# Expert scatter split by columns, residual loaded while routing, combination reordered

## The reference

```python
h = rms_norm(x1, g_pre_ffn) * (1.0 + sc2) + sh2
# group = top 1 of 4, experts = top 2 of the 8 in it, weights from two softmaxes
# the 4096 (token, expert) pairs are sorted by expert, each expert padded to rows of 128
hb = silu(xb @ w_gate[e]) * (xb @ w_up[e])       # one block of 128 rows, 1024 -> 256
yb = (hb @ w_down[e]) * weight                   # 256 -> 1024
y[token] += yb                                    # each token receives two rows
out = x1 + gt2 * rms_norm(y, g_post_ffn)
```

## Time and profile before

| | us |
|---|---|
| three runs | 1723.42, 1720.57, 1712.91 |
| median | 1720.57 |
| the profiled execution | 1719.75 |
| its span in the trace | 1717.9 |
| mixer | 0 to 1110 |
| routing | 1110 to 1149 |
| experts, to the last scatter's landing | 1149 to 1672.6 |
| combination | 1672.7 to 1717.9 |

### The profile page before, as it was taken

One profiled execution on the slowest core, in us unless ns is written; L12 is line 12 of the kernel. 1 busy time (PEld: TensorE's weight loads), 2 busy tenths in 40 slices (PEclk: granted clock), 3 DMA queues, 4 the chain that ended last, 5 costly groups with the idle time before them and its releaser, 6 DMA issues. The chain is left out here.

```text
span 1717.9 us, 23909 instructions
## 1 busy us (share of the span) xinstructions
PE 1551.8 (90%) x7453; PEld 1162.1 (68%) x7454; DVE 1234.7 (72%) x1928; ACT 867.7 (51%) x1512; POOL 373.9 (22%) x395
## 2 busy tenths in 40 slices
PE   2699987999999999999999999838799999999974
PEld 2588976688956788855889665425577667767741
DVE  4589676469884589885598954385778877887737
ACT  2323262333374423474324343325778877887746
POOL 1000000100001100001000011113566666665640
PEclk8699876999999999999999989859899999999996
DMA  9343334223332332332332343289999997789959
GB/s 331 116 147 99 98 122 172 70 78 98 99 107 90 98 96 92 121 99 74 87 98 74 122 123 111 84 275 348 304 297 311 302 312 224 201 245 285 282 108 383
DMA packets 200420, 291.25 MB, mean 170 GB/s; under 512 B 10558, under 2 KB 158171, under 8 KB 200346
## 3 DMA queue, kind: packets, MB, share of 16 engines
q1 hardware_dynamic: 170720, 197.15, 34.5%
q0 software_dynamic: 29360, 92.99, 19.8%
q10 hardware_dynamic: 266, 0.14, 0.0%
HBM read 240.42 MB, written 59.26 MB: 174 GB/s over the span
## 5 line engine op out<-in xcount | busy, mean ns | idle before, releaser
L934 DVE SCALAR_TENSOR_TENSOR cv<-u,taps,cv 128x512 f32<-128x512 f32 x480 | 321.8, 746 | 0.1
L1764 DVE TENSOR_TENSOR w_rest<-wgu,w_high 128x1024 fp32r<-128x1024 f32 x192 | 234.3, 1222 | 94.7 <-ACT w_high L1687 90.1
L1687 ACT ACTIVATE w_high<-wgu 128x1024 fp32r x192 | 202.1, 1054 | 106.2 <-PE pgu L1641 87.9
L488 PE MATMUL bank<-wo,yT 128*128 128x512 f32 x512 | 228.1, 602 | 2.5 <-ACT hT L664 2.5
L461 PE MATMUL bank<-hT_high,tiles_operand 128*128 128x512 f32 x512 | 201.0, 393 | 9.8 <-DVE hT_operand L907 8.5
L462 PE MATMUL bank<-hT_operand,tiles_operand 128*128 128x512 f32 x512 | 200.2, 391 | 0.0
L463 PE MATMUL bank<-hT_high,win_operand 128*128 128x512 f32 x512 | 200.1, 391 | 0.0
L488 PEld LDWEIGHTS bank<-wo,yT 128*128 128x128 f32 x512 | 97.2, 193 | 119.0 <-issue 119.0
L1651 PE MATMUL py<-wd,hTe 128*128 x384 | 172.6, 592 | 0.9 <-ACT yb L1714 0.9
L1639 PE MATMUL pgu<-w_high,x_high 128*128 128x512 f32 x384 | 156.2, 407 | 1.0 <-DVE x_rest L1779 1.0
L1640 PE MATMUL pgu<-w_rest,x_high 128*128 128x512 f32 x384 | 151.8, 395 | 0.0
(11 more groups left out here) (355 smaller groups left out, 2785.5 us busy)
## 6 DMA issues: line engine op xcount, KB each, us to landing
win<-w_in_in SPq DMA_DIRECT2D x64, 512.0 KB, 5.2
wgu<-w_gate_in SPq DMA_DIRECT2D x32, 1024.0 KB
wgu<-w_up_in SPq DMA_DIRECT2D x32, 1024.0 KB
wd<-w_down_in SPq DMA_DIRECT2D x32, 1024.0 KB
win<-w_in_in SPq DMA_DIRECT2D x16, 1024.0 KB, 5.1
wo<-w_ada_in POOLq DMA_DIRECT2D x6, 2048.0 KB, 9.3
y_dram<-zeros POOLq DMA_DIRECT2D x17, 512.0 KB, 5.1
tiles<-x_in POOLq DMA_DIRECT2D x16, 512.0 KB, 6.0
```

Of the source, the lines that this page charges most:

```text
L488: last = nc.tensor.matmul(out[:], yT[:, w % 2, k, :], wo[:, k, half * 512:(half + 1) * 512], start=(k == 0), stop=(k == KD - 1))
L934: ins = V.scalar_tensor_tensor(out=cv[:, j], in0=u[:, j, w:w + T], scalar=tap, in1=cv[:, j], op0=ALU.mult, op1=ALU.add)
L1687: A(w_high[:, QK * q:QK * q + QK, :], c.wgu[:, bass.ds(slot, 1), QK * q:QK * q + QK, :].rearrange("p a k n -> p (a k) n"), ACT.Copy).then_ ...
L1764: V.tensor_tensor(w_rest[:, part, :], c.wgu[:, bass.ds(slot, 1), part, :].rearrange("p a k n -> p (a k) n"), w_high[:, part, :].bitcast(F3 ...
```

## The change

The scatter of a block becomes two, of columns 0 to 511 and 512 to 1023. Each half has its own semaphore pair, so that it waits for its own half of `yb` and for the same half of the previous scatter. The y tensor is seen as rows of half the length, so a place becomes twice the row, or twice the row plus one. All eight pieces of x1 are started in routing, behind the first nine weight loads. In the combination the five PE tiles are 0, 1, 4, 7, 10 and tiles 0 and 1 are groups of their own.

```diff
@@ route_sync
-        load_residual(sp, ap, c, range(2))
+        load_residual(sp, ap, c, range(NTILES // 2))
@@ route_vector
-        L(V.tensor_scalar(c.block_place[:], c.block_token[:], beyond[:], None, ALU.min))
+        L(V.tensor_scalar(c.block_place[:, 0], c.block_token[:], beyond[:], None, ALU.min))
+        L(V.tensor_scalar(c.block_place[:, 0], c.block_place[:, 0], 1, None, ALU.arith_shift_left))
+        L(V.tensor_scalar(c.block_place[:, 1], c.block_place[:, 0], 1, None, ALU.bitwise_or))
@@ expert_stage
-    places, assigned = (sb(n, [P, 2], I32) for n in ("places", "assigned"))
+    places, assigned = sb("places", [P, 2, 2], I32), sb("assigned", [P, 2], I32)
+    y_halves = ap["y"].rearrange("r (h n) -> (r h) n", h=2)
-    y_stored = [sem("y_stored0"), sem("y_stored1")]
+    y_stored = [[sem(f"y_stored{s}{half}") for half in range(2)] for s in range(2)]
@@ serve, expert_sync
-            if known and r < 2:
-                load_residual(sp, ap, c, range(2 * r + 4, 2 * r + 6))
...
-        sp.wait_ge(x_turned, 4)
-        load_residual(sp, ap, c, range(2, 4))
@@ store
-            nc.gpsimd.tensor_copy(places[:, s:s + 1], c.block_place[:, bass.ds(b, 1)]).then_inc(place_copied, 1)
+            nc.gpsimd.tensor_copy(places[:, s], c.block_place[:, :, bass.ds(b, 1)].rearrange("p h a -> p (h a)")).then_inc(place_copied, 1)
             pool.wait_ge(place_copied, b + 1)
-            wait_apart(pool, y_saved, 2 * b + 3, pool_passed)
-            if before is not None:
-                wait_apart(pool, y_stored[1 - s], before, pool_passed)
-            pool.indirect_dma_start(ap["y"], bass.IndirectOffsetOnAxis(places[:, s:s + 1], 0), yb[:, s], None,
-                                    compute_op=ALU.add).then_inc(y_stored[s], 16)
+            for half in range(2):
+                wait_apart(pool, y_saved, 2 * b + 2 + half, pool_passed)
+                if before is not None:
+                    wait_apart(pool, y_stored[1 - s][half], before, pool_passed)
+                pool.indirect_dma_start(y_halves, bass.IndirectOffsetOnAxis(places[:, s, half:half + 1], 0),
+                                        yb[:, s, half * 512:(half + 1) * 512], None, compute_op=ALU.add).then_inc(y_stored[s][half], 16)
@@ save (ACT)
+            act.wait_ge(y_stored[s][half], 16 * times)
             if half == 0:
-                act.wait_ge(y_stored[s], 16 * times)
@@ combine_stage
-    ON_PE = (0, 3, 6, 9, 12)
-    GROUPS = [(0,)] + [(i, i + 1) for i in range(1, NTILES - 1, 2)] + [(NTILES - 1,)]
+    ON_PE = (0, 1, 4, 7, 10)
+    GROUPS = [(0,), (1,)] + [(i, i + 1) for i in range(2, NTILES, 2)]
-    STORE_ORDER = [1, 2, 0, 4, 5, 3, 7, 8, 6, 10, 11, 9, 13, 14, 12, 15]
-    SAVE_AFTER = {i: i + 2 for i in ON_PE}
+    STORE_ORDER = [2, 3, 0, 5, 1, 6, 8, 4, 9, 11, 12, 7, 13, 14, 10, 15]
+    SAVE_AFTER = {0: 5, 1: 7, 4: 9, 7: 11, 10: 15}
```

More of the change, by code:

```diff
@@ L1615, in expert_gpsimd @@
         for s in range(2):
-            wait_apart(pool, y_stored[s], n_rounds * 16 + 16, pool_passed)
+            for half in range(2):
+                wait_apart(pool, y_stored[s][half], n_rounds * 16 + 16, pool_passed)
             wait_apart(pool, xg_in[s], n_rounds * 16 + 32, pool_passed)
@@ L1854, in combine_sync @@
         for s in range(2):
-            wait_apart(sp, c.y_stored[s], n_rounds * 16 + 16, c.sp_passed)
+            for half in range(2):
+                wait_apart(sp, c.y_stored[s][half], n_rounds * 16 + 16, c.sp_passed)
         for i in range(NTILES):
@@ L1995, in build @@
             c.block_token, c.block_assign = eb("block_token", [P, TAB], I32), eb("block_assign", [P, TAB], I32)
-            c.block_place, c.row_weight = eb("block_place", [P, TAB], I32), eb("row_weight", [P, 2])
+            c.block_place, c.row_weight = eb("block_place", [P, 2, TAB], I32), eb("row_weight", [P, 2])
             c.weight_stored = c.sem("weight_stored")
```

## The result

| | us, median | lowest to highest | runs |
|---|---|---|---|
| before | 1720.38 | 1712.91 to 1724.27 | 8 |
| after | 1732.59 | 1725.48 to 1740.23 | 8 |

The ratio is 1.0080, interval 1.0058 to 1.0103: the change made the kernel 0.8% slower. The prediction said 1707, in 1695 to 1723: it pointed the other way, and the measured 1732.59 lies above its range. The profiled execution took 1735.93 us, 3.3 above its median, with a span of 1734.2. All ratios, here and in the experiments, leave out slow executions, whose cause isn't known: one of seven of e7 took 3178.97 us, one of seven of e9 2677.56, and one of the kernel before, run beside e5 to e8, 1761.83.

The account below looks back on a forecast made before the run. PE was taken to set the pace, 10.1 us a block. Terms -14.6 + 1.5 + 2.5 + 2.0 - 4.0 - 0.8 sum to -13.4, giving 1707 us from the median, range 1695 to 1723.

Parts of the forecast that it names:

- One such issue costs POOL 1.08 us: Expert loop, POOL: the further indexed DMA a block was priced at 1.08 us, making its cycle 10.3 against 10.1.
- the +2 that follows from it: Expert loop: two scatters a block were to cost +2 us in all, with ends -2.5 and +9.
- My end of +9: Expert loop: upper end of the two-scatter term, if POOL's cycle is 10.3 instead of 10.1 in all 44 rounds.
- The first rival: Expert loop: DVE holds the further issue and POOL becomes the bound; 1740 us, deciding from 0.35 a block; chance 0.13.
- The stall: Gap between the `down`s of blocks 2 and 3: earlier x1 loads take back 14.6 us less a remainder of 1.5.
- From a start at about 1184 it lands about 9.6 us later: Before block 4's rounding: rank 3's down load, started about 6.4 us earlier, lands near 1194 at 327 GB/s.
- the second rival's case: Before block 4's rounding: announcement stays late, down load needs nearly its 15 us, only SP's 6.4 gained; 1713; chance 0.20.
- Both signs that the prediction named for being wrong: Loop and stall: `down` to `down` over 10.4 us, or the wait before block 4's rounding above 5 us.
- The first fetch: Routing: rows fetched beside full queues land later, +2.2 us; with 0.6 for added DVE instructions, partly overlapped, +2.5 together.
- The end of the experts: Last save to the read of y: half scatters finish sooner, -4 us, ends -1.5 and -5.5; a half alone takes 4.4.
- The combination: After the read of y: new tile order and groups give -0.8 us in sum, ends -2 and +1.
- the 15.4 us that the terms beside the loop were to bring: Outside the loop: gain of 15.4 us from the other terms, used up if the loop loses 0.35 us a block.

Follow-up runs that it names:

- e7: The changed kernel with POOL's list reordered: copies of rows and places together, assignment copy between the scatter halves, weight fetch behind the second half; 1704.91 us.
- e9: e7 with SP announcing gate and up weights ahead of the wait for down weights; 1706.22 us.
- e5: The kernel before, scatter whole, plus one indexed fetch a block of 128 numbers that nobody reads; 1738.67 us.
- e8: e2 with SP announcing gate and up weights ahead of the wait for down weights; 1712.41 us.
- e4: The whole change with the scatter left in one piece; 1710.10 us.
- e10: The changed kernel with only the copy of the assignment moved between the two scatter halves; 1719.41 us.
- e2: The kernel before with only x1 loaded in routing; 1712.57 us.
- e6: The changed kernel without the weight fetch and its copy after the first two blocks, scatter halves kept; 1709.49 us.
- e11: e4 with the copies of rows and places together in POOL's list, scatter whole; 1707.55 us.

## Why the prediction was wrong

**The failed step is "One such issue costs POOL 1.08 us, the spacing from the scatter at 1339.00 to the copy behind it", and the +2 that follows from it.** The row measures when a *copy* may start behind an indexed DMA. The new instruction is an indexed DMA behind an indexed DMA, and the trace before had no such pair without a copy between. It starts 1.92 to 1.96 us later: the whole instruction, 1.6, and 0.30. A larger number stood in the same row, whose duration is 1.61, and I took the smaller for a price. The sum shows what that did: before, POOL's list without its waits for scatters took 8.7 us a block (10.1 less 55.2 in 40); with 1.08 it is 9.8, under PE's pace, and with 1.94 it is 10.7, over it. In the turns shown above no scatter waits for another, so no wait was left to absorb the 1.9: a turn without a longer copy takes 9.9 to 10.0, which is PE's pace, and one that a longer copy stretches, 11.2, is over it. The mean is 10.53. PE's five short waits for rows became 17, and 40 blocks cost 17.1 us. My end of +9 for this term was taken from the same wrong price. Of the 26.6 us between forecast (-13.4) and result (+13.2, without the mixer) the loop is 15.1.

**The first rival was right in its place and wrong in its price.** It said that POOL becomes the bound, from 0.35 us a block; the loop lost 0.43 (10.53 less 10.10). I had it rest on DVE's holds. They are there: the copy at 1448.99 ends at 1451.14, as DVE's subtraction of 1449.89 to 1451.11 does. But in the first turn, from 1436.53 to 1437.89, DVE read PSUM, and the second half came no sooner. And at the end of the experts DVE stands idle from 1672.2 to 1691.68, and two halves, at 1675.49 and 1677.39, are again 1.90 apart:

```profile
1691.68 2.58 DVE L1938 TENSOR_TENSOR scaled<-wgu,grow 128x1024 f32<-128x1024 f32 x2 [19.45 <-DMA wgu<-y_dram]
```

The Trainium skill, "SBUF — State Buffer", section "Who interferes with whom", says that a DVE instruction with two SBUF inputs contends with a GpSimd instruction that reads SBUF; the copy agrees with it, and the steady 1.9 us is something else. I gave the rival 0.13, arguing that 55.2 us of POOL's waits would go. They did go, to 9.5, a gain of 46 in 40 blocks or 1.1 each, and the issue took 1.9. The rest of the balance is holds that fell on other instructions: from 1236 to 1640 us the copy of `rows` took 1.09 us on average before and 0.26 after, that of `assigned` 0.86 and 1.28. How the 0.43 divides between the issue and the holds isn't shown, since no run takes DVE's holds away.

**The stall** came back by 7.05 in place of 13.1. The loads of x1 moved as foreseen and the announcement came earlier, but ACT still waited 8.85. The step that failed here is "From a start at about 1184 it lands about 9.6 us later". SP did start rank 3's down load 4.6 us earlier, counted from the first weight load (1188.63 less 1113.75, before 1190.12 less 1110.62), but the load itself stayed long: by the chains of waits it took 14.17 us in e7, 11.79 in e4 and 12.22 in e10, against 15.35 before. That is the second rival's case, in which only SP's head start is gained, and its -6.4 is close to the measured -7.05. (On the scale of the forecast's 1707 its time is 1714, not 1713.) The same edit with whole scatters (e2, e4) brings 10.5 to 10.6, so the halves seem to cost 3 here, as the gaps of e6 and e7, 17.91 and 17.54, do too; but e10, with halves and one copy moved, has 14.99, so the cause stays open. The announcement's cure gained nothing with halves (e9). Both signs that the prediction named for being wrong came: `down` to `down` over 10.4, and this wait over 5 us.

**The first fetch** was right: from its start at 1146.83 to PE's first turn at 1154.26 are 7.43 us, 2.1 more than in the earlier trace rows, predicted 2.2. The whole step is +1.5 of 2.5.

```profile
1146.83 1.11 POOL L1462 DMA_INDIRECT xg<-xn_dram,rows  x1 [0.97 <-POOL rows L1460]
```

**The end of the experts** was predicted at -4 and came at +1.1. POOL's rows show both sides of it:

```profile
1673.18 1.09 POOL L1579 DMA_INDIRECT row_weight<-weight_dram,assigned  x1 [0.89 <-POOL assigned L1577]
...
1675.49 1.59 POOL L1590 DMA_INDIRECT y_dram<-yb,places  x1 [1.02 <-issue]
1677.39 1.55 POOL L1590 DMA_INDIRECT y_dram<-yb,places  x1 [0.30 <-issue]
...
1681.00 1.55 POOL L1590 DMA_INDIRECT y_dram<-yb,places  x1 [1.86 <-DMA y_dram<-yb,places]
1683.45 1.54 POOL L1590 DMA_INDIRECT y_dram<-yb,places  x1 [0.90 <-DMA y_dram<-yb,places]
```

```profile
1676.53 1.26 ACT L1715 ACTIVATE yb<-py,row_weight 128x512 f32<-128x512 f32 x2 [4.25 <-DMA row_weight<-weight_dram,assigned]
```

The kernel before had started block 46's scatter here, 0.8 us after the `down` of block 47 (1658.07):

```profile
1658.86 1.59 POOL L1590 DMA_INDIRECT y_dram<-yb,places  x1 [3.14 <-DMA y_dram<-yb,places]
```

POOL now comes late: the `down` of block 47 starts at 1672.67, and block 46's halves follow it by 2.8 and 4.7 us. Behind them wait the halves of block 47. POOL also fetched block 47's weights only at 1673.18, and ACT's last saves waited 4.25 us for them, most of it beside PE's `down`: the last save ends 5.1 us after that `down` starts, before 4.4 (1662.49). The last half by itself is cheaper than a whole scatter: y is read 4.88 us after its start, against 6.21. I had put it at 4.4, a saving of 1.8; it is 1.3. The Trainium skill, "DMA: Bandwidth & Descriptors", section "Anatomy of one DMA", would make the saving an estimated 0.6, so the measurement lies between. Where POOL keeps up, e7 needs 12.10 us from `down` 47 to the read of y, and e11, not split, 14.16: the split is worth 2.1 there, half of the 4.

**The combination** gave nothing. ACT's and DVE's rows:

```profile
1698.46 1.28 DVE L1945 SCALAR_TENSOR_TENSOR wgu<-wgu,rstd,grow 128x1024 f32<-128x1024 f32 x1 [4.20 <-ACT rstd L1889]
...
1712.58 1.29 DVE L1945 SCALAR_TENSOR_TENSOR wgu<-wgu,rstd,grow 128x1024 f32<-128x1024 f32 x1 [1.94 <-ACT rstd L1889]
```

```profile
1708.05 0.60 ACT L1879 ACTIVATE x_all<-pgu 128x512 f32<-128x512 f32 x1 [2.51 <-PE pgu L1918]
```

The first scaled tile comes 10.1 us after the reading begins, as foreseen (10.5), and DVE's product fills part of the hole, 2.58 us for two. The +0.6 itself says little: from the read of y to the end the five kernels with the old order take 44.5 to 45.2 us in their traces, and the nine with the new one 44.6 to 46.0. A new hole of 1.94 stands at 1712.58: ACT, in its list, had waited 2.51 for PE's sum before it could square the next tiles. I had costed the squares of the start and the end and not the places of the saves between them.

Of the 15.4 us that the terms beside the loop were to bring, 3.9 came (-7.05 + 1.5 + 1.1 + 0.6). With the loop at its predicted +2, the kernel would still have been within a few microseconds of the one before.

## What to carry to other kernels

Before an instruction is added to an engine's list, price it by the spacing between two starts of its own kind in that place; if no such pair stands in the trace, put at least its full duration into the sum (here 1.61, and even that was short of the measured 1.9). An engine that stands in waits may still be little below the pace of the bound engine (here 8.7 of 10.1 us), so add up its list without the waits, and compare with the block. A cheap probe for "issue or transfer" is the same instruction with next to no data.

## What the runs showed of the hardware

- A scatter that follows a scatter in POOL's list starts 1.9 us after it (1.96, 1.92, and 1.90 with DVE idle), with rows of 2 KB: the first one's duration and 0.30. A small copy behind it starts after 1.0. In e5 two fetches of 128 numbers lie 2.37 us apart where the first took 2.07, and 1.37 where it took 1.07 (at 1237.52). A copy put between two scatters can cost next to nothing (e7 1638.98 and 1640.96: 1.98).
- An indexed DMA that waits for the copy of its own indices starts 0.85 to 1.07 us after that copy's end; with a second copy between, the wait is shared.
- Scatters of rows of half the length: 36,272 packets for 29,360, the same 93.0 MB, and q0's time goes from 340 us (19.8% of 1717.9) to 364 (21.0% of 1734.2), 7% more; in e7 it is 353 (20.7% of 1702.9), 4% more.
- In a stretch with DMA full (share 1.04 to 1.07), an order that cured one wait left the sum as it was to the hundredth: 67.54 us for six blocks in e7 and e9. With whole scatters it took 2.7 off (e2, e8).
